# Separate dependencies for each column of the ConvFFN history, with its copy in issued one column ahead, in a two-layer hybrid decoder step on eight cores

## The reference, cut to what matters

```
def _conv_ffn(h, prev, w_up, conv_w, conv_b, w_down):
    u = h @ w_up                                   # 1024 -> 8192
    u, conv_state = _causal_dwconv(u, prev, conv_w, conv_b)   # width 3, along the tokens
    val, gate = jnp.split(u, 2, axis=-1)           # 4096 + 4096
    return (jax.nn.gelu(gate, approximate=True) * val) @ w_down, conv_state
```

## Time and profile before

| quantity | value |
|---|---|
| median of 2 runs | 4215.81 us (4166.43 and 4265.18) |
| profiled execution | 4203.05 us, span of its slowest core 4201.5 us |
| spans of the eight cores | 4156.2 to 4201.5 us |
| busy share TensorE / VectorE / ScalarE / GpSimd | 69% / 49% / 53% / 19% |
| mean granted TensorE clock by core | 0.783 to 0.793 |

### The profile page before, as it was taken

The page is one execution under the profiler, slowest core; times in us unless marked ns, Lnnn a source line. Parts: engine busy times, 40 slices in busy tenths (PEclk is TensorE's granted clock), DMA queues, the critical chain, the costliest instruction groups (busy, mean ns, idle before and its releaser), DMA issues.

```text
span 4201.5 us, 58031 instructions; the slowest of 8 cores (4156.2 to 4201.5 us)
## 1 busy us (share of the span) xinstructions
PE 2916.0 (69%) x15052; PEld 1365.9 (33%) x15302; DVE 2050.1 (49%) x3903; ACT 2245.5 (53%) x4567; POOL 806.9 (19%) x2042
## 2 busy tenths in 40 slices
PE   5167867348777548982797478955897289855897
PEld 3033434124333223431343133422343134312343
DVE  2533761542672354816382446545571638344481
ACT  3563653564563464727383556546573647346471
POOL 1000220011121002610161013400250015200150
PEclk9568988658888768985898678976898589866787
DMA  8305455415247306870568336940687155821563
GB/s 151 70 12 102 83 89 91 83 34 101 54 86 138 78 2 113 147 122 11 101 121 160 50 53 108 155 76 15 109 156 130 26 101 104 138 53 21 96 125 71
DMA packets 114477, 371.48 MB, mean 88 GB/s; under 512 B 14232, under 2 KB 29160, under 8 KB 113640
## 3 DMA queue, kind: packets, MB, share of 16 engines
q0 software_dynamic: 94816, 330.41, 45.7%
q1 hardware_dynamic: 19336, 37.33, 3.3%
HBM read 685.83 MB, written 20.35 MB: 168 GB/s over the span
## 4 chain that ended last, share of the span: by engine, by line
PE 55%; DVE 20%; ACT 12%; issue 9%; DMA 2%; DVEq 1%; SPq 1%; ACTq 0%; POOL 0%; POOLq 0%
PE ps L515 36%; PE ps L974 6%; PE ps L991 6%; DVE xc L790 3%; DVE x L506 2%; ACT Sbuf L558 2%; DVE mbuf L504 2%; PE ps L584 2%; PE ps L615 2%; DVE xc L847 2%; DVE h L495 1%; DVE cvs L1121 1%; DVE ii L844 1%; PE ps L477 1%; DVE cvg L1080 1%
## 5 line engine op out<-in xcount | busy, mean ns | idle before, releaser
L515 PE MATMUL ps<-h,wslot 128*128 128x512 bf16 (+1 forms) x5414 | 1222.8, 386 | 79.7 <-DVE h L495 56.0
L515 PEld LDWEIGHTS ps<-h,wslot 128*128 128x128 bf16 x5536 | 531.3, 101 | 770.5 <-issue 266.6
L515 PE MATMUL ps<-A,wslot 128*128 128x512 bf16 (+1 forms) x2508 | 495.1, 360 | 40.5 <-DVE A L1087 36.5
L1080 DVE SCALAR_TENSOR_TENSOR cvv<-Uv,smalls,cvv 128x512 f32<-128x512 f32 x512 | 383.6, 749 | 103.2 <-ACT cvv L1074 72.8
L1080 DVE SCALAR_TENSOR_TENSOR cvg<-Ug,smalls,cvg 128x512 f32<-128x512 f32 x512 | 383.2, 749 | 49.1 <-ACT cvg L1074 16.1
L504 DVE TENSOR_TENSOR mbuf<-mbuf,rstd 128x512 f32<-128x512 f32 (+1 forms) x128 | 89.8, 702 | 640.3 <-ACT rstd L482 640.3
L515 PEld LDWEIGHTS ps<-A,wslot 128*128 128x128 bf16 x2560 | 225.3, 102 | 309.4 <-issue 131.1
L811 PE MATMUL ps<-xcb,gatesw 128*128 128x512 bf16 (+1 forms) x155 | 59.4, 544 | 374.0 <-ACT xcb L801 374.0
L584 PE MATMUL ps<-identb,Pn 128*128 128x128 bf16 (+1 forms) x624 | 108.0, 261 | 244.7 <-ACT Pn L568 179.5
L994 ACT ACTIVATE sgA<-ps 128x512 f32<-128x512 f32 (+1 forms) x160 | 83.6, 522 | 352.7 <-PE ps L974 302.5
L974 PE MATMUL ps<-h,wslot 128*128 128x512 bf16 (+1 forms) x1240 | 262.8, 354 | 3.8 <-issue 2.0
(11 more groups left out here) (168 smaller groups left out, 4500.2 us busy)
## 6 DMA issues: line engine op xcount, KB each, us to landing
wslot<-wup_r POOLq DMA_DIRECT2D x256, 512.0 KB, 10.2
wslot<-win_r POOLq DMA_DIRECT2D x144, 512.0 KB, 8.0
wslot<-wdn_r POOLq DMA_DIRECT2D x128, 512.0 KB, 10.7
wslot<-wlo_r POOLq DMA_DIRECT2D x32, 512.0 KB, 7.6
wslot<-wao_r POOLq DMA_DIRECT2D x32, 512.0 KB, 9.9
wslot<-wout_r POOLq DMA_DIRECT2D x32, 512.0 KB, 10.3
tokx<-xp SPq DMA_DIRECT2D x4, 2048.0 KB, 18.4
yp<-tok SPq DMA_DIRECT2D x4, 2048.0 KB, 6.8
```

Of the source, the lines that this page charges most:

```text
L515: S.add("pe", lambda e, b=b, c0=c0, n=n, k=k: e.matmul(ps_t[b][:, 0:n], wt[:, k, col:col + 128], rhs[:, k, c0:c0 + n], start=(k == 0), sto ...
L1080: S.add("dve", lambda e, Ub=Ub, cvb=cvb, jj=jj, k=k: e.scalar_tensor_tensor(out=cvb[:, 0:TP], in0=Ub[:, 62 + k:62 + k + TP], scalar=wsc(k, ...
```

## The change: what it does

1. The key ("ffnhist", l) becomes one key per layer and column, ("dram", "ffnhist", l, jj). A "dram" key stands only for itself.
2. The history fill of a buffer is no longer issued for the column at hand. It is issued for the next column, j+1, into the next buffer of the rotation, ahead of the copy out of column j; for column 0 it is issued in place.
3. In pass 0 the copies from FH to Us move from the head of the block to just ahead of ScalarE's copy to Us, one for each half.
4. At the start, tokx is loaded inside do_pass(0), after the constants on the SP queue; the weight stream doesn't wait for it; and the two gate loads are queued ahead of the weight blocks.

```
-    S.add("sp", lambda e: e.dma_start(out=tokx[:], in_=xp[0:TP, :]...), writes=["tokx"], dsem="xin")
-    W = WStream(S, nc, seq, wslots, first_reads=["tokx"])
     for l in range(DEPTH):
         S.add("pool", lambda e, l=l: e.dma_start(out=gatesw[l][:], in_=gates_r[l]), ...)
+    W = WStream(S, nc, seq, wslots)
...
+        if p == 0:
+            S.add("sp", lambda e, p=p: e.dma_start(out=tokx[:], ...), writes=["tokx"], dsem="xin")
...
+            def hist_in(Un, ui_, jj_):
+                Ub_ = (Uv if Un == "Uv" else Ug)[ui_]
+                if p == 0:
+                    S.add("pool", lambda e: e.memset(Ub_[:, 62:64], 0.0), writes=[(Un, ui_, "h")])
+                else:
+                    S.add("pool", lambda e: e.tensor_copy(out=Ub_[:, 62:64], in_=ffnhist[l][:, jj_, :]),
+                          reads=[("dram", "ffnhist", l, jj_)], writes=[(Un, ui_, "h")])
...
-                if has_s:
-                    for half in range(2):
-                        S.add("pool", ... out=Us[half][...0:2], in_=FH[...] ..., reads=["FH"], writes=[("Us", half)])
...
-                        if p == 0:
-                            S.add("pool", lambda e, Ub=Ub: e.memset(Ub[:, 62:64], 0.0), writes=[UH])
-                        else:
-                            S.add("pool", lambda e, Ub=Ub, jj=jj: e.tensor_copy(out=Ub[:, 62:64], in_=ffnhist[l][:, jj, :]),
-                                  reads=[("ffnhist", l)], writes=[UH])
+                        if j == 0:
+                            hist_in(Un, ui, jj)
+                        if j + 1 < 32:
+                            hist_in(Un, (ui + 1) % 3, jj + 1)
...
                         S.add("pool", lambda e, Ub=Ub, jj=jj: e.tensor_copy(out=ffnhist[l][:, jj, :], in_=Ub[:, 62 + TP:64 + TP]),
-                              reads=[UB], writes=[("ffnhist", l)])
+                              reads=[UB], writes=[("dram", "ffnhist", l, jj)])
...
                         S.add("pe", mm, reads=[wres_] + HR, writes=[PSR(b)])
+                        S.add("pool", lambda e, Uh=Uh, jj0=jj0: e.tensor_copy(out=Uh[:, :, :, 0:2], in_=FH[:, jj0:jj0 + 4, :]...),
+                              reads=["FH"], writes=[("Us", half)])
                         S.add("act", lambda e, Uh=Uh, b=b: e.copy(out=Uh[:, :, :, 2:6], ...), writes=[PSR(b), ("Us", half)])
```

More of the change, by code:

```diff
@@ L190, with __init__ @@
 class WStream:
-    def __init__(self, S, nc, seq, slots, first_reads=()):
+    def __init__(self, S, nc, seq, slots):
         self.S = S
@@ L194, in __init__ @@
         self.slots = slots
-        self.first_reads = list(first_reads)
         self.next_dma = 0
@@ L211, in fn @@
                         for i in range(nd)]
-            self.S.add("pool", fn, reads=(self.first_reads if n == 0 else ()), writes=[("w", sl)], dsem=("w", sl), ndma=nd)
+            self.S.add("pool", fn, writes=[("w", sl)], dsem=("w", sl), ndma=nd)
             self.next_dma += 1
@@ L419, in build @@
                 seq.append(((p,) + key, t[l * n + key[2]], 4096))
-    S.add("sp", lambda e: e.dma_start(out=tokx[:], in_=xp[0:TP, :].rearrange("(j r) d -> r j d", r=128)), writes=["tokx"], dsem="xin")
-    W = WStream(S, nc, seq, wslots, first_reads=["tokx"])
     for l in range(DEPTH):
         S.add("pool", lambda e, l=l: e.dma_start(out=gatesw[l][:], in_=gates_r[l]), writes=[("gatesw", l)], dsem=("gw", l))
+    W = WStream(S, nc, seq, wslots)
     S.add("sp", lambda e: e.dma_start(out=identf[:], in_=ident_d), writes=["identf"], dsem="c0")
@@ L636, in do_pass @@
         XRs = XR[:, :, 3 + TP:3 + TP + NB * 7].rearrange("p c (b k) -> p c b k", k=7)
+        if p == 0:
+            S.add("sp", lambda e, p=p: e.dma_start(out=tokx[:], in_=xp[p * TP:(p + 1) * TP, :].rearrange("(j r) d -> r j d", r=128)),
+                  writes=["tokx"], dsem="xin")
         if has_s:
@@ L1107, in do_layer @@
                         S.add("pe", mm, reads=[wres_] + HR, writes=[PSR(b)])
+                        S.add("pool", lambda e, Uh=Uh, jj0=jj0: e.tensor_copy(out=Uh[:, :, :, 0:2], in_=FH[:, jj0:jj0 + 4, :].rearrange("p c (b k) -> p c b k", k=2)),
+                              reads=["FH"], writes=[("Us", half)])
                         S.add("act", lambda e, Uh=Uh, b=b: e.copy(out=Uh[:, :, :, 2:6], in_=ps_t[b][:, 0:4 * NS].rearrange("p (c b t) -> p c b t", c=4, t=4)),
@@ L1139, in do_layer @@
                                                           in_=ffnhist[l][:].rearrange("p c k -> p k c")),
-                      reads=[("ffnhist", l)], writes=["pst"])
+                      reads=[("dram", "ffnhist", l, q_) for q_ in range(64)], writes=["pst"])
                 transpose_out(lambda k: pst[:, 0:128], [128], [o_pf[l].rearrange("k (c p) -> (k c) p", p=128)], ["pst"], "pf")
```

## The result

The changed kernel takes 1.0068 times the time of before, 95% interval [1.0042, 1.0094]: 28 us of 4175, between 17.5 and 39. The medians are 4219.22 us (26 runs) and 4174.99 us (25 runs of before); each holds runs of the chip's slower state, which the ratio leaves out. I had forecast 12 us more than the profiled time. The direction was right and the size is over twice that.

What follows compares the result with a forecast made beforehand. The prediction took VectorE to bound the up-projection and the chain through the toks load to bound the start. It summed 4203.05 + 17.5 (start) - 6 (keys) = 4214.5, say 4215 us, range 4165 to 4270.

Steps and rivals of the forecast that it cites:

- The start (item 4): Program start: weight and gate loads moving early beside the SP queue delay toks; +17.5 us, bounds +3 and +29.
- the ratio of turns: Start: SP and GpSimd queues share by packets, about 1.22 to 1, so 1430 packets let 1170 others pass; toks +21 us.
- all 12 transfers ahead: Start, third reading: all 12 GpSimd queue loads go before toks, 38.5 us, toks near 53: +32 us.
- The discount of 3.5 us for the recurrent state: Start: the recurrent state load is no longer beside weights, so 3.5 us is won, 4.1 at most.
- The keys (item 1): Up-projection: GpSimd's history copy waits vanish, gaining between 0 and about 10 us; 6 us taken back.
- The prefetch (item 2): Up-projection: the earlier copy in must wait for VectorE's read of its buffer, but this is met on arrival; 0 us.
- The Us copies (item 3): Pass 0 sample history copies, FH to Us: ScalarE now waits for them, but with 1.1 us margin per block; 0 us.
- The clock at the start: First transposes after longer idleness might run at the 1.2 GHz level; 9 us at most, 0 taken.
- D: Up-projection: the key per column does nothing, the start alone remains; 4221 us, chance 0.15.
- A: Start costs next to nothing, as the SP queue keeps its share by bytes; 4200 us, chance 0.22.
- B: Up-projection: the prefetched copy's wait for VectorE holds GpSimd at 256 columns; slower by over 2%, 4476 us, chance 0.04.
- C: Up-projection: GpSimd is a hidden pacer, relief gains 0.4 us a column; faster by over 2%, 4118 us, chance 0.04.

Runs made afterwards that it cites:

- the history edits alone: The change with the start of before (keys per column, prefetch of the copy in, moved sample history copy), against the kernel before: ratio 1.0018 [0.9978, 1.0059].
- the keys-alone run: The kernel before with own keys per column alone and every history fill done twice: ratio 1.0267 [1.0119, 1.0416], stage 137.2 us.
- the dose: The kernel before with the first two weight blocks running free, the other three and the gates waiting for toks: ratio 1.0038 [1.0023, 1.0053].
- the whole edits under load: All history edits of the change, start of before, every history fill done twice, against the kernel before: ratio 0.998 [0.9937, 1.0023], stage 122.8 us.

## Why the prediction was wrong

- **The start (item 4), +17.5 us: right mechanism, mis-sized term; it measured 23.** Three things in it were off. First, I let SP's remaining 3.49 MB run alone at 286 GB/s, 12.2 us; alone they end at 20.0 us, that is 15 us. The rate came from the window up to 14 us, with large packets; in the run whose weights wait for toks SP's queue moves 2.62 MB in 707 packets from 5 to 14 us and 0.89 MB in 726 packets from 14 to 20 us. Second, the ratio of turns: 1.22 to 1 from two windows, but 1378 to 1321, 1.04 to 1, over the whole 41 us, so 1321 packets passed and not 1170. Both windows hold a stretch before the weight queue had begun: 116 packets to 8 from 16 to 17 us, 76 to 4 from 1308 to 1309 us; from 1310 to 1312 us it was 70 to 65. Third, the reading "all 12 transfers ahead" is added up wrongly: 5 + 12.2 + 38.5 - 1 is 54.7 us and not 53, which would move only the upper bound. The discount of 3.5 us for the recurrent state held about: toks is 26.2 us later, the first copy 23.0.
- **The rule of the Trainium skill** that I weighed (DMA: Bandwidth & Descriptors, "Queues, rings and completion order", turns between queues) gives, as the estimate in the prediction from even turns, toks near 48 us and the start at +24. The trace agrees: turns of 1.04 to 1, toks at 46.4 us and +23 us.
- **The keys (item 1), -6 us: this step failed.** I took the waits that the wait view puts down to GpSimd (5.5 us of VectorE, 3.1 of ScalarE) as time on the path. They did go (VectorE's to 0.9 us, ScalarE's to nothing that shows), and four of the five distances between up-projections stayed within 0.3 us with the whole change and 0.6 us with the history edits alone, in both directions (the fifth takes one of two values within one kernel). The stage got 0.4 us shorter at most. So VectorE's delays of 0.2 to 0.5 us are made up within the stage or behind it; by what, no run shows. I had also put the waits of GpSimd's copies under the keys alone: besides the 21.4 us of the copies in there were 25.1 us of copies out waiting for a fill, and these go only with the prefetch, as the keys-alone run shows.
- **The prefetch (item 2), 0 us: right.** Inside a stage no copy in waits for VectorE in any amount that shows (0.2 us in the group of L1052).
- **The Us copies (item 3), 0 us: right**, as far as the history edits alone gain or lose nothing; they were not tried by themselves.
- **The clock at the start, 0 taken:** right. The first group of transposes takes 1.08 us after 44 us of idleness, as before (1.09, rows 5), and the granted clock is 1.00, the 2.4 GHz level, from 30 to 44 us and from 47 to 60 us.
- **The sum:** 23 + 0 = 23 us, against my 17.5 - 6 = 11.5. The measured 28 is 16.5 above that: 5.5 from the start, 6 from the keys, and 5 for which I know no stage. The interval of 17.5 to 39 us has 23 inside, and the shortest run of each kernel, 4172.27 and 4149.39 us, are 22.9 us apart.
- **The rivals.** D (the keys gain nothing) is the one that came nearest, with 17.5 us where 28 was measured (23 by the start), though not for its reason: GpSimd does wait less, only nobody needs it. A (shares by bytes) is refuted. B did not occur. C, GpSimd as hidden pacer, was false as put and closer than its 0.04 says: with one more copy per part it does set the pace, and costs 108 us. Its sum of 3.7 us per column was near the 3.54 read above, but its gain of 0.4 us a column had no room, since VectorE's column takes 3.63 us. My 3.9 us was the stage divided by 32, its start and end included.

## What to carry to other kernels

A wait on an engine that is idle anyway may be what keeps its transfers off the path: before a prefetch is let loose, ask which transfer the chain waits for and count the packets that will take turns with it. A small wait in the wait view is not a gain until the stage's own floor is below it, and an engine that the chain never names can still be just under the pace; doubling a part of its work shows it. A false dependency is gone only when every pair of neighbours in the queue is free of it; here, under load, finer keys and another order were each worth 1.5 us of 138.7 by themselves and 15.9 together.

## What the runs showed of the hardware beyond that

- Two DMA queues with work share the engines packet by packet, large or small: 210 to 206 packets at 0.75 to 0.15 MB, and 150 to 151 at 0.54 to 0.61 MB. Each packet of the weight queue cost the other 0.022 us in the dose and 0.020 us in the whole change.
- Single cores can lose 27 to 30 us in one stretch of one execution, at a lower granted clock. In before's profile core 6 needs 483.9 us from the seventh to the last of its up-projections (3480.2 to 3964.1 us), core 0 454.4 us (3496.4 to 3950.8). Core 7 needs 481.7 us. The granted clock (the figure behind five engines) over 480 us of that stretch, core 6 and core 0:

```profile
3480.00:3960.00 480.00, 350.26 (x1444) 148.30 (x1470) 233.35 (x402) 249.33 (x461) 107.40 (x238) 0.76 0.50 87
...
3480.00:3960.00 480.00, 340.03 (x1496) 147.00 (x1525) 251.70 (x428) 259.83 (x477) 109.61 (x246) 0.80 0.49 87
```

  Without these 29.5 us before's span would lie below that of the slower kernel.
- A GpSimd copy of 128x2 elements takes 0.18 us or up to some 0.75 us. In the timeline of the whole edits under load the long ones lie beside a VectorE instruction and end with it: a copy out from 2116.37 us takes 0.72 and ends at 2117.09, the first of two scalar_tensor_tensor of 0.75 us from 2116.31 ends at 2117.06, and the copy of 0.18 us at 2117.03 lies between the two. One completion wait adds 0.19 us.
